# The level products of a triangular inverse: whole 128x128 products or tiles of the array

## The reference

```
def step(S, inp):                       # per head, over 512 tokens
    r_t, w_t, k_t, v_t, a_t, b_t = inp
    sa = jnp.einsum('bhij,bhj->bhi', S, a_t)
    S = S * w_t[:, :, None, :] + sa[..., None] * b_t[:, :, None, :] + v_t[..., None] * k_t[:, :, None, :]
    return S, jnp.einsum('bhij,bhj->bhi', S, r_t)
```

## Time and profile before

| | |
|---|---|
| median of three runs | 3118.72 us (3115.41 to 3122.08) |
| profiled execution, its span | 3114.6 us |
| matrix engine busy | 3019.7 us, 97% |
| weight loads busy | 2423.6 us, 78% |
| VectorE, ScalarE, POOL busy | 1697.0, 1213.4, 283.4 us (54%, 39%, 9%) |
| matrix operations, and as many loads | 15418 |
| mean granted clock | 0.990 |

### The profile page before, as it was taken

The page is one execution under the profiler, slowest core; times in us unless marked ns, Lnnn a source line. Parts: engine busy times, 40 slices in busy tenths (PEclk is TensorE's granted clock), DMA queues, the critical chain, the costliest instruction groups (busy, mean ns, idle before and its releaser), DMA issues.

```text
span 3114.6 us, 39362 instructions
## 1 busy us (share of the span) xinstructions
PE 3019.7 (97%) x15418; PEld 2423.6 (78%) x15418; DVE 1697.0 (54%) x2880; ACT 1213.4 (39%) x2131; POOL 283.4 (9%) x517
## 2 busy tenths in 40 slices
PE   9999999999999999999999999999999999999897
PEld 7778787878788877777778868787787887868786
DVE  6554545454543336556553364656666666565647
ACT  5443434343433324434343333434444343434422
POOL 0110101010100000000000002202022020212001
PEclk9999999999999999999999999999999999999999
DMA  4222222222243321221233322212222131224334
GB/s 164 82 77 84 78 82 82 82 82 82 82 135 131 106 88 62 68 75 62 68 122 134 122 85 80 83 55 90 75 70 90 61 97 56 89 72 140 135 129 155
DMA packets 86007, 288.99 MB, mean 93 GB/s; under 512 B 12080, under 2 KB 12720, under 8 KB 85568
## 3 DMA queue, kind: packets, MB, share of 16 engines
q1 hardware_dynamic: 69696, 243.66, 23.9%
q0 software_dynamic: 16128, 42.81, 4.5%
HBM read 261.13 MB, written 25.17 MB: 92 GB/s over the span
## 4 chain that ended last, share of the span: by engine, by line
PE 83%; DVE 9%; ACT 4%; issue 2%; DMA 1%; POOL 1%; DVEq 0%; ACTq 0%; SPq 0%; POOLq 0%
PE bank L280 14%; PE bank L282 14%; PE bank L281 14%; PE bank L284 7%; PE bank L286 7%; PE bank L285 7%; PE bank L1370 2%; PE bank L1301 1%; PE bank L1306 1%; DVE mc_split L736 1%; PE bank L337 1%; PE bank L317 1%; ACT mc_split L568 1%; PE bank L472 1%; PE bank L485 1%
## 5 line engine op out<-in xcount | busy, mean ns | idle before, releaser
L280 PE MATMUL bank<-ma_split,mc_split 128*128 128x512 f32 x2304 | 957.1, 415 | 12.7 <-DVE ma_split L890 7.7
L736 DVE TENSOR_TENSOR mc_split<-mc,mc_split 128x1024 fp32r<-128x1024 f32 x434 | 534.9, 1233 | 790.1 <-ACT mc_split L568 789.0
L282 PE MATMUL bank<-ma_split,mc_split 128*128 128x512 f32 x2304 | 905.8, 393 | 0.0
L281 PE MATMUL bank<-ma_split,mc_split 128*128 128x512 f32 x2304 | 902.4, 392 | 0.0
L568 ACT ACTIVATE mc_split<-mc 128x1024 fp32r<-128x1024 f32 x434 | 457.8, 1056 | 658.5 <-PE bank L284 349.6
L280 PEld LDWEIGHTS bank<-ma_split,mc_split 128*128 128x128 f32 x2304 | 436.8, 190 | 121.5 <-issue 49.1
L282 PEld LDWEIGHTS bank<-ma_split,mc_split 128*128 128x128 f32 x2304 | 434.6, 189 | 97.0
L281 PEld LDWEIGHTS bank<-ma_split,mc_split 128*128 128x128 f32 x2304 | 436.9, 190 | 78.7 <-issue 4.4
L284 PE MATMUL bank<-mc_split,ma_split 128*128 128x512 f32 x576 | 230.2, 400 | 5.0 <-DVE mb L1780 3.4
L286 PE MATMUL bank<-mc_split,ma_split 128*128 128x512 f32 x576 | 225.3, 391 | 0.0
L285 PE MATMUL bank<-mc_split,ma_split 128*128 128x512 f32 x576 | 224.7, 390 | 0.0
(11 more groups left out here) (366 smaller groups left out, 3732.6 us busy)
## 6 DMA issues: line engine op xcount, KB each, us to landing
mc<-in_w SPq DMA_DIRECT2D x434, 512.0 KB, 3.5
x<-mc POOLq DMA_DIRECT2D x8, 1024.0 KB, 5.2
y<-mb_split SPq DMA_DIRECT2D x28, 256.0 KB, 2.5
ma_split<-y POOLq DMA_DIRECT2D x28, 256.0 KB, 4.5
mb<-in_xt SPq DMA_DIRECT2D x8, 512.0 KB, 9.5
mc<-in_x POOLq DMA_DIRECT2D x4, 1024.0 KB, 5.7
mc<-x POOLq DMA_DIRECT2D x4, 1024.0 KB, 6.5
mats<-mc POOLq DMA_DIRECT2D x32, 128.0 KB, 2.2
```

Source lines behind the costliest of these rows:

```text
L280: mm = pe.matmul(banks[j][:], wh[:, c], act_hi[:, kt, :], start=(kt == 0), stop=False)
L281: pe.matmul(banks[j][:], wl[:, c], act_hi[:, kt, :], start=False, stop=False)
L282: last = pe.matmul(banks[j][:], wh[:, c], act_lo[:, kt, :], start=False, stop=(kt == KT - 1))
L736: dve.tensor_tensor(w_low[:, s % NR, :, :], w_raw[:, s % NR, :, :], w_high[:, s % NH, :, :].bitcast(F32), ALU.subtract).then_inc(w_lo, 1)
```

## The change

Only the products of W and T change. A new function names the tiles of a level. On levels 4 and 5 each block of the diagonal, 32 x 32 or 64 x 64, becomes a product of its own, with the block's partitions as rows and outputs, on the tile of the array that belongs to them. On level 6 the block is the whole matrix, of which one quarter is wanted: W takes the earlier half of the rows into the later half of the outputs, and T the other way. Copies, waits and masks stay as they are; a half of a group still signals once, after its last product.

```
+            def level_tiles(lv, downward):
+
+                if lv == LEVELS - 1:
+                    earlier, later = slice(0, P // 2), slice(P // 2, P)
+                    return [(0, earlier, later) if downward else (0, later, earlier)]
+                size = 2 << lv
+                return [(j, *[slice(j * size, (j + 1) * size)] * 2) for j in range(P // size)]
...
                             for q in mats:
-                                mm = pe.matmul(to[:, q % 4], m8[:, q, 0:P], halves(xw, lv)[0][:, q], start=True, stop=True)
+                                for j, rows, outs in level_tiles(lv, True):
+                                    mm = pe.matmul(to[outs, q % 4, j], m8[rows, q, outs], halves(xw, lv)[0][rows, q, j],
+                                                   start=True, stop=True)
...
                             for q in mats:
-                                mm = pe.matmul(to[:, q % 4], xw[:, q, :], halves(xt, lv)[1][:, q], start=True, stop=True)
+                                for j, rows, outs in level_tiles(lv, False):
+                                    mm = pe.matmul(to[outs, q % 4, j], xw[rows, q, outs], halves(xt, lv)[1][rows, q, j],
+                                                   start=True, stop=True)
```

## The result

The changed kernel takes 3089.1 us (median of 4 runs, 3087.1 to 3090.9) where the kernel before takes 3118.8 on the same chip: ratio 0.9902, 95% interval 0.9889 to 0.9914. That is 29.8 us less; 25 were forecast (3094), and the range was 3081 to 3119. The profiled execution went from 3114.6 to 3086.2 us, 28.4 less. Two executions of the experiments fell far behind all others of their kernel (3722 us in the version with whole and tiled products in turn, 8614 us in the one with 64x64 tiles on level 4), and the medians of these two versions are of the other executions.

The account below looks back on a forecast made before the run. The matrix engine was taken as the bound (83% of the chain, busy 97%). Group gains of 31 us, less 2 and 4 us of returning waits, gave 25 us: from 3118.7 to 3094 us, range 3081 to 3119.

Parts of the forecast that it names:

- The old price: W and T groups before the change: 1.79 us each from outside, 48 groups, 85.9 us of the span.
- The price of narrow loads: Weight loads on tiles: 0.057 us per record for 64 columns, 0.031 for 32, against 0.11 for 128.
- Overlap of diagonal tiles: Levels 4 and 5: diagonal tiles writing one bank work at the same time, giving groups of 0.85 and 1.27 us.
- Rival 2: Levels 4 and 5: diagonal tiles writing into one bank don't overlap; 8 us slower, 3126; chance 0.11.
- The floor: Matrix engine: a least distance between record starts, taken as 0.055 us; the change loses from 0.035 on.
- Rival 3: Levels 4 and 5: record starts at least 0.055 us apart, 31 us slower; chance 0.13.
- Entering and leaving: Each tiled W or T group: switching layout in and out, 0.35 us at level 4, 0.36 at 5, 0.38 at 6.
- What comes back: Gain lost again as waiting of the matrix engine: 2 us behind the groups plus 4 us in the stage.
- The first part: X groups behind T: 0.2 to 0.4 us of waiting for DVE's copies at 5 or 6 places, 2 us.
- The second part: Stage waits, as L1281's loads waiting for DVE: chains beside the levels are late already; 4 us, a guess.
- Rival 1: Stage waits for DVE and others swallow nearly all the gain; 3110 to 3119 us; chance 0.12.
- The clock: Matrix engine: full clock through the level stretch, half in short stretches; a change there stays under 1.7 us.

Follow-up runs that it names:

- the order by tile: Changed kernel with its W and T products reordered, for each tile its four systems instead of for each system its tiles: 3103.0 us (0.9953).
- the other recurrence: Changed kernel plus HGRN's level products, levels 0 to 4, cut into tiles of 128 rows x 32 columns: 3080.1 us (0.9877).

## Why the prediction was right

- **The old price.** 1.79 us a group, 48 groups. The runs that leave groups whole show it again (1.79).
- **The price of narrow loads.** 136 and 108 ns were read for 64 and 32 columns, 134 and 105 are there. The pace on one tile can now be read from the loads: (1.00 - 0.134) / 15 = 0.058 us at level 6 for the 0.057 taken, and 0.033 at level 4 for the extrapolated 0.031. Sixteen records at these paces leave 0.33 us of the level 4 group and 0.35 of the level 6 group for going in and out, where 0.35 and 0.38 were taken. So the two terms were off by 0.02 to 0.03 in opposite ways, and that their sum met 0.86 with 0.85 is in part luck.
- **Overlap of diagonal tiles.** It was carried over from two pairs of tiles and held for four. Rival 2 (8 us slower) and its rule are answered: 64 records in 0.73 us, while one tile after the other would need 1.98 by the prediction's pace, and the same records in runs of eight on a tile took 1.50. The Trainium skill, "TensorEngine Tiling (Array Packing)", Restrictions and Gotchas, says that different row tiles can't use one PSUM bank at the same time. Here they do, each on its own 32 partitions; the trace decides. The prediction read the Trainium skill, "PSUM — Partial Sum Buffer", section PSUM bank collisions raise a hardware error, as speaking of one quadrant only; the error that it reports as measured is of one quadrant, but it also quotes the rule for the whole bank. No run takes the overlap away altogether, the order by tile only in part.
- **The floor.** Rival 3 took 0.055 us between starts; a record starts every 0.008. The Trainium skill, "TensorE: Matmul & The Clock Gate", Part 1, gives 25 ns as the least distance; over tiles that work side by side the trace shows a third of it, and the trace decides. On one tile no run here has starts closer than 0.03 us.
- **Entering and leaving.** Forecast 0.35 to 0.38 with the exposed load, and the three group prices came out at 0.86, 1.25 and 1.27 against 0.85, 1.27 and 1.29. The sum of the three gains is 1.99 against 1.96, 32 us against 31. The prediction called this cost new and counted the exposed load of the plain product as part of it; that load stood almost as exposed before the change (0.48 and 0.31 us against 0.50 and 0.33). It did the sum no harm, since both prices were taken from outside.
- **What comes back** is the term that was too large: 6 us forecast, 2.6 in the trace. The first part, 2 us at five or six X places, was 0.9 at a single one. It rested on a wrong reading of the air. In the code each half of X waits only for the copy of its own half (`T{lv - 1}{p}`), and the first of the two copies ended near 1908.84, 0.7 us ahead of X's first load, not 0.3; and read as the prediction read it, 0.3 to 0.4 us of air is at 4 of the 16 places. It also took the whole shortening of the second half off the air, though where DVE is free its copy starts earlier with the products, and the air stays: in unit 3 the second copy of level 4 ended 0.61 us ahead of X's first product before and 0.63 after. Only where DVE's queue is full (L1714 in unit 0) is it lost, and there it is what W and T lost together, 1.87 us. The second part, 4 us put on the waits of the stage, was 2.5 at L1251 and L1370; at L1281, the line it was read from, the matrix engine waits for DVE 6.3 us before and after.
- **Rival 1** had its place and its mechanism right, but the share was 8% of the 31 us in the idle time and 15% at 64 us. In the other recurrence it was about 4 of 13 us by the medians, of which 2.9 are seen as longer waits for DVE: there the shortened product itself stands between two of DVE's copies. That last reason is read from the waits and was not tested by a run of its own.
- **The clock** stayed at a mean of 0.990 in both profiles, as assumed.

## What to carry to other kernels

Small f32 products with 128 x 128 weights are bound by loading the weights (0.11 us a record here, where 64 columns stream in 0.053), so cut the columns of the weights to what is wanted, give neighbouring tiles to neighbours in the order, and reckon 0.3 us for each time in and out of the tiled layout (0.28 to 0.35 here). Price such a group from the starts around it, in the trace of the kernel before; other lines with tiles of any kind give the pace, the overlap and the drain. Then count the idle time of the bounding engine before and after: what it grew by is what the chains behind took back.

## What the runs showed of the hardware

- Cutting rows is worth nothing here: on level 4, 128 x 32 tiles took 0.85 to 0.89 us where 32 x 32 took 0.85 to 0.86, though the four share all rows.
- The order of issue decides how much tiles overlap. By runs on one tile of two, four and eight records a level 4 group took 0.86, 0.95 and 1.62 us. That a tile takes about three records ahead of the queue is an estimate from these.
- Going in and out of the tiled layout cost 0.28 us between small products and 0.33 to 0.35 between large ones. Part of it may be shared: the four groups beside L1249 (L1241 before, 64 rows) gained 0.13 to 0.15 us more than the others of their level.
- Over 64 records on four tiles in turn a record started every 0.008 us, and every 0.033 on each tile.
